# Latent attention: each head's scores, maxima and exponentials put ahead of the next head's products, rotations, squares and roots

## The reference, cut to what matters

```
q = (rms_norm(c_q) @ w_uq).reshape(b, s, 4, 96);  kv = (rms_norm(c_kv) @ w_ukv).reshape(b, s, 4, 128)
k = concat(kv[..., :64], k_r broadcast to the heads);  v = kv[..., 64:]
q, k = rms_norm(q), rms_norm(k)             # over the 96 features of a head
q, k = rope on the last 32 features of each # x1*cos - x2*sin, x2*cos + x1*sin
logits = q @ k.T * 96**-0.5, masked by chunks of 64
o = softmax(logits) @ v                      # then rms_norm over 64, the mix with w_out
```

## Time and profile before

| | us |
|---|---|
| median of 3 runs | 3176.36 (3174.09 to 3176.57) |
| the profiled execution | 3174.81 |
| its span in the trace | 3173.0 |
| TensorE busy | 3069.1 (97%) |
| VectorE busy | 1644.8 (52%) |
| ScalarE busy | 1434.9 (45%) |
| mean granted TensorE clock | 0.989 |

### The profile page before, as it was taken

The page is one execution under the profiler, slowest core; times in us unless marked ns, Lnnn a source line. Parts: engine busy times, 40 slices in busy tenths (PEclk is TensorE's granted clock), DMA queues, the critical chain, the costliest instruction groups (busy, mean ns, idle before and its releaser), DMA issues.

```text
span 3173.0 us, 43952 instructions
## 1 busy us (share of the span) xinstructions
PE 3069.1 (97%) x13727; PEld 2430.3 (77%) x13727; DVE 1644.8 (52%) x2441; ACT 1434.9 (45%) x2100; POOL 736.7 (23%) x508
## 2 busy tenths in 40 slices
PE   8999999999999999999999989999999988999998
PEld 6888888788887777888867767788887776778887
DVE  6544445575665977574657573511125756441113
ACT  4333333443333675343356764522345666542224
POOL 2333323100000000000023213244443220334444
PEclk9999999999999999999999999999999999999999
DMA  5333322333333232433222112133332220223334
GB/s 160 95 104 93 88 81 73 95 114 99 97 93 93 60 106 80 135 96 96 75 65 67 59 37 67 47 93 93 98 119 69 57 66 21 67 73 93 93 93 132
DMA packets 490394, 273.00 MB, mean 86 GB/s; under 512 B 9550, under 2 KB 479766, under 8 KB 489848
## 3 DMA queue, kind: packets, MB, share of 16 engines
q1 hardware_dynamic: 485576, 264.45, 29.0%
q10 hardware_dynamic: 4656, 6.58, 0.6%
HBM read 267.69 MB, written 12.21 MB: 88 GB/s over the span
## 4 chain that ended last, share of the span: by engine, by line
issue 56%; PE 30%; POOL 11%; DVE 2%; ACT 1%; POOLq 0%; ACTq 0%; DMA 0%; DVEq 0%
PE acc L753 9%; PE acc L754 9%; PE acc L759 8%; POOL s_w_lo L722 5%; POOL s_w_lo L721 5%; PE acc L756 1%; PE wide L785 1%; PE misc L754 0%; PE misc L753 0%; PE misc L759 0%; DVE s_sc L2610 0%; PE wide L753 0%; POOLq L111 0%; PE wide L754 0%; ACTq L1670 0%
## 5 line engine op out<-in xcount | busy, mean ns | idle before, releaser
L753 PE MATMUL acc<-s_h_hi,s_w_hi 128*128 128x512 f32 (+1 forms) x1920 | 787.8, 410 | 15.5 <-DVE s_h_lo L3053 9.2
L754 PE MATMUL acc<-s_h_lo,s_w_hi 128*128 128x512 f32 (+1 forms) x1920 | 753.2, 392 | 0.0
L721 POOL TENSOR_TENSOR s_w_lo<-s_raw,s_w_hi 128x512 fp32r<-128x512 f32 x212 | 274.9, 1297 | 2020.9 <-ACT s_w_hi L1623 2020.0
L759 PE MATMUL acc<-s_h_hi,s_w_lo 128*128 128x512 f32 (+1 forms) x1680 | 659.4, 393 | 0.0
L1623 ACT ACTIVATE s_w_hi<-s_raw 128x1024 fp32r<-128x1024 f32 x386 | 409.3, 1060 | 386.1 <-DVE s_x L3308 210.8
L753 PEld LDWEIGHTS acc<-s_h_hi,s_w_hi 128*128 128x128 f32 x1920 | 363.3, 189 | 115.6 <-issue 19.9
L754 PEld LDWEIGHTS acc<-s_h_lo,s_w_hi 128*128 128x128 f32 x1920 | 363.7, 189 | 87.5 <-issue 12.3
L759 PEld LDWEIGHTS acc<-s_h_hi,s_w_lo 128*128 128x128 f32 x1680 | 317.6, 189 | 73.1
L704 POOL TENSOR_TENSOR s_w_lo<-s_raw,s_w_hi 128x1024 fp32r<-128x1024 f32 x80 | 191.5, 2394 | 406.2 <-ACT s_w_hi L1623 404.6
L722 POOL TENSOR_TENSOR s_w_lo<-s_raw,s_w_hi 128x512 fp32r<-128x512 f32 x212 | 279.0, 1316 | 0.0
L753 PE MATMUL acc<-s_hid_hi,s_w_hi 128*128 128x512 f32 x704 | 278.1, 395 | 0.0
(11 more groups left out here) (498 smaller groups left out, 5416.4 us busy)
## 6 DMA issues: line engine op xcount, KB each, us to landing
s_raw<-w_ff SPq DMA_DIRECT2D x128, 512.0 KB, 4.0
s_raw<-ffn_w_up SPq DMA_DIRECT2D x96, 512.0 KB, 3.9
s_raw<-attn_w_qkv SPq DMA_DIRECT2D x72, 512.0 KB, 3.8
s_raw<-ffn_w_down SPq DMA_DIRECT2D x48, 512.0 KB, 4.0
s_raw<-w_in SPq DMA_DIRECT2D x48, 512.0 KB, 4.0
s_raw<-lru_w_in SPq DMA_DIRECT2D x16, 512.0 KB, 4.0
s_raw<-w_out SPq DMA_DIRECT2D x16, 512.0 KB, 4.0
s_bd<-bias_by_head SPq DMA_DIRECT2D x24, 256.0 KB, 5.0
```

The source lines that it names most:

```text
L721: pool.tensor_tensor(w_lo_b[s][:, 0:h, :], raw_b[s][:, 0:h, :], w_hi_b[s][:, 0:h, :].bitcast(F32), ALU.subtract)
L753: mm(out, ahi, bhi, start=start, stop=False, **kw)
L754: mm(out, ahi, blo, start=False, stop=False, **kw)
L759: mm(out, alo, bhi, start=False, stop=stop, **kw)
```

## The change

The order of steps in the loop over the heads is changed on three engines. No instruction is added or taken away, no semaphore wait is written anew, no buffer is changed, and the waits that stand in the moved steps move with them. TensorE's scores of head h go ahead of the products of head h+1, and `query_sum` leaves the middle of the scores for the place before `mla_sums`. ACT's exponentials of head h go ahead of the squares and the queries' root of head h+1. DVE's maxima of head h go ahead of `mla_evict` of head h+1.

```
                         mm(o[:, 0:w], q_lo2[:, r], k_hi2[:, 0:w], start=False, stop=True,
                            skip_group_check=True).then_inc(sems["wide_full"], 1)
                         count("wide_full")
-                        if q == 2 and h < HEADS_2 - 1:
-                            query_sum()
...
                 for h in range(HEADS_2):
+                    mla_scores(h)
                     if h < HEADS_2 - 1:
                         mla_products(h + 1)
-                    mla_scores(h)
                     if h == HEADS_2 - 1:
                         head_sum(HALVES)
                     if h:
                         mla_weigh(h - 1, TT)
                     if h < HEADS_2 - 1:
+                        query_sum()
                         mla_sums()
                     mla_turn()
...
                 for h in range(HEADS_2):
-                    if h < HEADS_2 - 1:
-                        mla_squares(h + 1)
-                        head_rstd(MLA_W, MLA_W)
                     for q in range(TT):
                         count("wide_full")
                         act.wait_ge(sems["nmax_ready"], count("nmax_ready"))
...
                     if h < HEADS_2 - 1:
+                        mla_squares(h + 1)
+                        head_rstd(MLA_W, MLA_W)
                         mla_hi(h + 1)
...
                 for h in range(HEADS_2):
-                    if h < HEADS_2 - 1:
-                        mla_evict()
                     for q in range(TT):
                         nc.vector.tensor_reduce(sm[:, q:q + 1], next_wide()[:, 0:(q + 1) * P], AX_X, ALU.max,
                                                 negate=True).then_inc(sems["nmax_ready"], 1)
                         count("nmax_ready")
+                    if h < HEADS_2 - 1:
+                        mla_evict()
```

## The result

| | before | changed |
|---|---|---|
| median of 5 runs, us | 3175.17 (3174.09 to 3176.57) | 3189.30 (3189.03 to 3191.51) |
| the profiled execution's span, us | 3173.0 | 3187.5 |
| mean granted TensorE clock | 0.989 | 0.985 |

A forecast was written before the change was run, and what follows sets the result against it. VectorE's row of steps was taken to bound a head. Two layers at +2.7 us (5.4) and four slow heads at 3.1 (12.4) gave +17.8 us on 3174.81, 3192.6; predicted 3193 us, range 3180 to 3199.

The forecast's parts named there:

- Part 1: Head 0: its scores start 2.14 us sooner, but head 1's scores start only 1.1 us sooner than before.
- Part 2: Heads 1 and 2: evictions and roots come later, so each takes 14.55 us instead of 12.68, +1.9 us.
- Part 3: TensorE's gaps ahead of scores, 2.2 and 2.9 us: the clock falls, 3.1 us for each slow head 1 or 2.
- Rival A: Main forecast, clock low in three or four of the four heads: 3189 to 3196 us; chance 0.68.
- Rival B: Periods grow but the clock holds in these heads; +5.4 us and at most one slow head, 3180 to 3183; chance 0.14.
- Rival C: Scores' chain goes ahead, the other head's work fills the holes: -3.9 us a layer, 3167 us; chance 0.05.
- Rival D: Hand-overs cost more (+2.4 a head); clock also falls ahead of head 3's turn or stays low inside head 0: 3197 to 3202; chance 0.13.

The follow-up runs named there:

- the two filled kernels: Unread matmuls fill TensorE's gaps: changed kernel, 9 and 12 behind the turns of heads 0 to 2, 3175.96 us; kernel before, 12 behind head 2's turn, 3171.54 us.

## Why the prediction was right

I forecast 3193 us (3180 to 3199) and 3189.3 was measured; by the terms of the sum:

- **Part 1, head 0.** Forecast: head 1's scores start 13.6 us after head 0's. Measured 13.49. The new head 0 keeps 1.2 us of the 2.14 (forecast 1.1).
- **Part 2, a middle head at 1.00.** Forecast 14.55 us, measured 14.65: eviction at T+5.43 (5.45 measured), first scaling at T+10.85 (10.96: 1884.88 - 1873.92), with 0.61 us of waiting for the keys' root where I had 0.45. Order, both layers: forecast 5.4, measured 5.4 by the two filled kernels.
- **Part 3, the gaps.** Forecast 2.2 and 2.9 us, measured 2.33 and 3.06. The end of the turn was added up wrongly: the four terms give T+11.8 and not 11.6. It came out at T+11.6 all the same (1888.57 - 3.06 - 1873.92 = 11.59), because the ten transposes took 1.3 us and not 1.4. The price of a slow head: forecast 3.1, measured 3.13 and 2.96.
- **How many heads fall.** This is the term that was off. I took four at 3.1, 12.4 us. Measured: 0, 1.6, 3.1, 3.0, which is 7.7. Head 3, for which I took 0, pays 0.5 in each layer, because its clock stays low for longer (0.64 over 13.14 us, against 0.74 over 12.65). Together 8.7. Nothing in the rows said which heads would be spared, and the range, 3180 to 3199, held every count from none to four: that the time fell into it does not speak for the count of four. With the loop moved by 1.3 us the four heads fell as forecast, and that one run took 3194.9 us, 2.6 of them for the added matmuls.

The Trainium skill, in "TensorE: Matmul & The Clock Gate", section "HAM oscillation — how this bites in real kernels", has a loop with a stall in its body pay for the clock on every turn. The prediction called its case just this one, which goes too far: the waits of the page's loop are some 3 to 5 us for transfers, the gaps here 2.33 and 3.06. The second layer agrees with it all the same (0.80, 0.79, 0.63), head 1 of the first does not (1.00). The measured heads decide: with gaps of this size a turn can pay, and not each does.

Rival A is what came, at the lower end of its range. Rival B needed the clock to hold in heads 1 and 2; it held in one of four. Rival C fell with the first eviction: it waits for the square behind the exponentials, as written against it. Its idea can be had, though, when squares and products stay ahead: then a middle head does run in 12.55 us, and head 0 in 11.49 where its clock holds. Rival D did not come: a middle head costs 2.0 us more and not 2.4, and the clock fell neither in head 0 nor in the gap ahead of head 3's turn. It named a real danger, though: in five of the experiments the clock did fall in head 0.

## What to carry to other kernels

Where three engines each run a written list, a step that is moved ahead delays all that it passes. Ask who waits for that: here two squares of 0.65 us, passed by 2.9 us of exponentials, held up the engine that bounds the head. Look at what fills an engine's wait before you move it away; work that looks free in a gap may be what keeps TensorE's clock at its full level. Filling one gap can move the slow stretch to the next, so judge a fill by the whole time and not by the head that it mends. And when a change opens gaps of 1.5 to 3 us on TensorE, price the slow stretch behind them from a row of the trace, and expect the count of such stretches, not their price, to be the unsure term.

## What the runs showed of the hardware that was not expected

- In the run with the gaps cut in half, a gap of 1.53 us behind five matmuls of 512 columns was followed by the low clock, and the next of 1.52 us was not. In the kernel before, a gap of 2.24 us was not the earlier trace rows.
- The clock may fall after the gap is over. In head 2 of the changed kernel's first layer it does so some 1.7 us into the scores, with 3.4 us at the low level to follow; in head 1 of the second layer 0.4 us into them, with 6.8 us to follow; ahead of head 3 it falls inside the gap and stays low for over 10 us. The first of these:

```profile
1888.57:1890.00 1.43, 1.43 (x12) 1.43 (x13) 1.43 (x4) 0.60 (x1) 0.00 (x0) 1.00 0.00 0
1890.00:1891.00 1.00, 1.00 (x6) 1.00 (x6) 0.49 (x2) 0.69 (x3) 0.00 (x0) 0.63 0.00 0
...
1893.00:1894.00 1.00, 1.00 (x5) 0.69 (x4) 0.47 (x1) 0.50 (x1) 0.00 (x0) 0.66 0.00 0
```

- The two traced executions of the changed program show the same falls in the same heads. In the one run with the loop moved by 1.3 us in each layer one head more fell and another stayed slow for longer, and the time was 5.6 us longer: 3.7 us more in the heads, 2.6 for the added matmuls, and other stretches 0.7 us shorter together.
